# Head norm of a recurrent mixer: the bonus tiles loaded during the scan, gated by GpSimd and VectorE, their shift added by ScalarE

## The reference

```python
sa = einsum('bhij,bhj->bhi', state, kk_t)
state = state * w_t - sa * b_t + v_t * k_t           # one step per token
y_t = einsum('bhij,bhj->bhi', state, r_t)
...
y = (y - mean) * rsqrt(var + GN_EPS) * ln_w + ln_b    # head norm, per token and head
bonus = sum(r * k * r_k) * v                          # per head
y = y + bonus
return (y * silu(gate)) @ w_out
```

## Time and profile before

| what | value |
|---|---|
| time, median of 3 runs | 1241.23 us (1240.56 to 1241.37) |
| profiled execution: its own time, its span | 1244.49 us, 1242.7 us |
| TensorE, weight loads busy | 94%, 73% of the span |
| VectorE, ScalarE, GpSimd busy | 61%, 50%, 39% |
| TensorE's granted clock, mean over the span | 0.968 |
| DMA, mean | 96 GB/s |

### The profile page before, as it was taken

The page is one execution under the profiler, slowest core; times in us unless marked ns, Lnnn a source line. Parts: engine busy times, 40 slices in busy tenths (PEclk is TensorE's granted clock), DMA queues, the critical chain, the costliest instruction groups (busy, mean ns, idle before and its releaser), DMA issues.

```text
span 1242.7 us, 19541 instructions
## 1 busy us (share of the span) xinstructions
PE 1166.4 (94%) x7570; PEld 902.0 (73%) x7570; DVE 753.6 (61%) x1179; ACT 620.0 (50%) x1034; POOL 485.5 (39%) x391
## 2 busy tenths in 40 slices
PE   5899899998986999899999998999999999999997
PEld 4665667787872778677777776877888888867666
DVE  4775997894458346467666665274295234557763
ACT  4767453634553445466556464363122244465655
POOL 1432334456650444333323343443554445532321
PEclk9999899998896999899999999999999999999988
DMA  7742244536113253212222222522333333222111
GB/s 239 250 118 68 62 109 136 153 93 158 43 63 114 68 178 103 68 52 70 66 69 68 68 69 84 153 86 85 86 102 102 88 99 102 85 70 67 51 35 68
DMA packets 198941, 119.49 MB, mean 96 GB/s; under 512 B 27773, under 2 KB 187206, under 8 KB 198598
## 3 DMA queue, kind: packets, MB, share of 16 engines
q1 hardware_dynamic: 196256, 115.95, 32.1%
q10 hardware_dynamic: 2598, 2.33, 0.6%
HBM read 103.06 MB, written 15.20 MB: 95 GB/s over the span
## 4 chain that ended last, share of the span: by engine, by line
PE 41%; issue 30%; POOL 13%; DVE 12%; ACT 2%; DMA 1%; POOLq 0%; SPq 0%; ACTq 0%; DVEq 0%
POOL b_w_lo L562 13%; PE banks L645 10%; PE banks L647 10%; PE banks L646 10%; DVE b_problems L2129 1%; DVE b_sum_squares L2127 1%; PE banks L652 1%; PE banks L1220 1%; DVE b_a_lo L1989 1%; PE banks L893 1%; DVE b_suffix L2580 1%; PE banks L1248 1%; DMA b_spread_heads<-spread_heads 1%; PE banks L912 1%; DVE b_sum_squares L2062 1%
## 5 line engine op out<-in xcount | busy, mean ns | idle before, releaser
L562 POOL TENSOR_TENSOR b_w_lo<-b_w_raw,b_w_hi 128x512 fp32r<-128x512 f32 x320 | 429.5, 1363 | 711.6 <-ACT b_w_hi L1318 711.4
L645 PE MATMUL banks<-b_a_lo,b_w_hi 128*128 128x512 f32 x1280 | 527.4, 412 | 21.1 <-POOL b_w_lo L562 8.3
L647 PE MATMUL banks<-b_a_hi,b_w_lo 128*128 128x512 f32 x1280 | 508.3, 397 | 0.0
L646 PE MATMUL banks<-b_a_hi,b_w_hi 128*128 128x512 f32 x1280 | 507.2, 396 | 0.0
L645 PEld LDWEIGHTS banks<-b_a_lo,b_w_hi 128*128 128x128 f32 x1280 | 245.1, 191 | 101.8 <-issue 21.6
L1318 ACT ACTIVATE b_w_hi<-b_w_raw 128x1024 fp32r<-128x1024 f32 x160 | 168.8, 1055 | 250.3 <-PE banks L647 244.9
L647 PEld LDWEIGHTS banks<-b_a_hi,b_w_lo 128*128 128x128 f32 x1280 | 244.9, 191 | 53.7
L646 PEld LDWEIGHTS banks<-b_a_hi,b_w_hi 128*128 128x128 f32 x1280 | 245.8, 192 | 44.7
L1725 ACT ACTIVATE b_exps<-banks,b_stats 128x128 f32<-128x128 f32 (+3 forms) x64 | 33.2, 524 | 61.1 <-DVE b_stats L2370 61.1
L1659 ACT ACTIVATE b_a_hi<-b_x_t,b_params 128x512 fp32r<-128x512 f32 x48 | 33.9, 719 | 54.1 <-DVE b_x_t L2255 53.6
L2255 DVE TENSOR_TENSOR b_x_t<-b_x_t,banks 128x512 f32<-128x512 f32 x32 | 22.0, 687 | 60.2 <-PE banks L647 60.2
(11 more groups left out here) (314 smaller groups left out, 1513.7 us busy)
## 6 DMA issues: line engine op xcount, KB each, us to landing
b_w_raw<-rw_w_in SPq DMA_DIRECT2D x32, 512.0 KB, 4.4
b_w_raw<-da_w_in SPq DMA_DIRECT2D x32, 512.0 KB, 4.0
b_w_raw<-w_in_a SPq DMA_DIRECT2D x32, 512.0 KB, 4.0
b_w_raw<-pe_w_gate SPq DMA_DIRECT2D x16, 512.0 KB, 3.9
d_ple<-b_ple_out SPq DMA_DIRECT2D x16, 256.0 KB, 4.7
b_w_raw<-rw_w_out SPq DMA_DIRECT2D x8, 512.0 KB, 4.8
b_ple_in<-d_ple SPq DMA_DIRECT2D x2, 2048.0 KB, 10.4
b_w_raw<-da_w_out SPq DMA_DIRECT2D x8, 512.0 KB, 4.0
```

What stands on the lines that cost most here:

```text
L562: m = pool.tensor_tensor(WLO[:, u % 2, ks], WRAW[:, u, ks], WHI[:, u % 2, ks].bitcast(F32), ALU.subtract)
L645: pe.matmul(dst, hi, a_lo[:, k_act, :], start=first, stop=False)
L646: pe.matmul(dst, hi, a_hi[:, k_act, :], start=False, stop=False)
L647: return pe.matmul(dst, lo, a_hi[:, k_act, :], start=False, stop=last)
```

## The change

Four things change together.

1. **ScalarE adds the norm's shift** to a bonus tile in `bonus_out`, with one activation in place, before the tile is written to DRAM. It waits for its own activation before it issues the write.
2. **The bonus tiles are loaded during the scan**, one by one, into buffers of the scan that are no longer read: tiles 0 to 5 over the blocks of chunks 0 to 5 (`b_blocks`), tiles 6 and 7 over half of `b_nk_rows`. SP waits for TensorE's products of chunks 3, 5 and 5 before them. The one transfer of 2 MB behind the scan is gone.
3. **GpSimd gates tiles 0 to 3**: three in the iteration of chunk 5, one in that of chunk 6.
4. **VectorE gates tiles 4 to 7**, with a multiplication alone, in front of its wait for the roots. The loop over tiles has no bonus operation any more.

```diff
--- before.py
+++ after.py
@@ -279,8 +279,9 @@
-    BVT, SPREADH2, SPREADHR2, RK2, RKS2, RKC2 = phase([
-        ("bonus_v", [P, NT, TOK]), ("spread_heads2", [P, 2, P]), ("spread_heads2_r", [P, 2, P], F32R),
+    GATED = 4
+    SPREADH2, SPREADHR2, RK2, RKS2, RKC2 = phase([
+        ("spread_heads2", [P, 2, P]), ("spread_heads2_r", [P, 2, P], F32R),
...
+    def bonus_home(j):
+
+        at = TRI0[:, j] if j < 2 else TRI1[:, j - 2] if j < 6 else NKR[:, 1, 4 * (j - 6):4 * (j - 6) + 4]
+        return at.rearrange("p j t -> p (j t)") if j < 6 else at.rearrange("p j h d -> p (j h d)")
...
+        def load_bonus(j):
+            sp.dma_start(bonus_home(j), D_BV[j]).then_inc(sem(f"bonus_in{j // 4}"), 16)
+
+        sp.wait_ge(sem("u_mm"), 4)
+        for j in range(4):
+            load_bonus(j)
+        sp.wait_ge(sem("u_mm"), 6)
+        for j in range(4, 6):
+            load_bonus(j)
+        sp.wait_ge(sem("s_mm"), 6)
+        for j in range(6, NT):
+            load_bonus(j)
         sp.wait_ge(sem("v_placed"), 2 * 2 * NC)
         sp.dma_start(XT[:, :, :], D_XT.rearrange("j p t -> p j t")).then_inc(sem("x_spilled"), 16)
         sp.wait_ge(sem("y_even"), 2 * NC)
         sp.wait_ge(sem("y_odd"), 2 * NC)
-        sp.dma_start(BVT[:, :, :], D_BV.rearrange("j p t -> p j t")).then_inc(sem("gn_in"), 16)
...
+        def gate_bonus(j):
+            pool.wait_ge(sem(f"bonus_in{j // 4}"), 64)
+            pool.tensor_tensor(bonus_home(j), bonus_home(j), GT[:, j, :], ALU.mult).then_inc(sem("bonus_gated"), 1)
+            pool.wait_ge(sem("bonus_gated"), j + 1)
...
+            if c == NC - 3:
+                for j in range(3):
+                    gate_bonus(j)
+            if c == NC - 2:
+                gate_bonus(3)
...
         def bonus_out(j):
             act.wait_ge(sem("bonus_v"), j + 1)
+            own.step(act.activation(TMP[:, 2 + j % 2, :], TMP[:, 2 + j % 2, :], ACT.Identity, bias=prm(LN_B, j)))
             act.dma_start(D_BV[j], TMP[:, 2 + j % 2, :]).then_inc(sem(f"bv_out{j % 2}"), 16)
...
-        act.wait_ge(sem("gn_in"), 32)
+        act.wait_ge(sem("gn_in"), 16)
...
         def gated_bonus(j):
-            own.step(stt(out=BVT[:, j, :], in0=BVT[:, j, :], scalar=prm(LN_B, j), in1=GT[:, j, :], op0=ALU.add, op1=ALU.mult))
+            own.step(tt(bonus_home(j), bonus_home(j), GT[:, j, :], ALU.mult))
...
-            tt(YT[:, j, :], YT[:, j, :], BVT[:, j, :], ALU.add).then_inc(sem("gn_done"), 1)
-
-        dve.wait_ge(sem("gn_in"), 32)
-        for j in range(4):
-            gated_bonus(j)
+            tt(YT[:, j, :], YT[:, j, :], bonus_home(j), ALU.add).then_inc(sem("gn_done"), 1)
+
+        dve.wait_ge(sem("bonus_in1"), 64)
+        for j in range(GATED, NT):
+            gated_bonus(j)
+        dve.wait_ge(sem("bonus_gated"), GATED)
...
         for k in range(NT):
-            if k + 4 < NT:
-                gated_bonus(k + 4)
             if k + 2 < NT:
                 gn_scale(k + 2)
```

## The result

The changed kernel takes 1245.66 us (median of 15 executions, 1237.8 to 1250.3) where the kernel before takes 1239.5 (15, 1233.8 to 1241.9): ratio 1.0038, interval 1.0024 to 1.0051, 4.7 us slower. (The 4.7 us are the ratio's 0.38%; the two medians lie 6.2 us apart.) The forecast was 1240.5 with a range from 1237.6 to 1243.4. A repeat of both gave 1.0038 again (1.0021 to 1.0056).

The account below looks back on a forecast made before the run. TensorE, busy 94%, bounds dense stages; VectorE's solve ends last in value and gate slots, and VectorE bounds the head norm. 2.2 + 0.4 + 0.1 - 3.4 = -0.7 us from 1241.2 gives 1240.5, range 1237.6 to 1243.4.

Parts of the forecast that it names:

- Part 1: Head norm: VectorE bounds it, and moving bonus work out shortens it; 3.4 us gain taken, between 2.1 and 4.5.
- (a): Head norm, before the roots' wait: four plain multiplications start earlier and run shorter; combination of the roots 0.62 us earlier.
- (b): Head norm, loop over tiles: four bonus operations of 0.78 us leave VectorE's loop, saving 3.12 us.
- (c): Head norm, TensorE's output projection: earlier low parts gain 2.1 to 4.5 us by where the clock rises; 3.4 taken.
- Part 2: Value and gate slots: activation and write issue hold ScalarE's queue; solve 2.2 us later, 0.4 more at the scan's start.
- The late write: Value slots: write 0 goes out 2.8 us later but lands in time at 2.1 us; priced at nothing.
- Rival B: Value slots: late writes take 5.7 us and delay VectorE's bonus 4 by 2.9; 1243.4 or 1244.7 us; chance 0.10.
- Part 3: Scan: bonus loads find SP's queue nearly free, GpSimd's gatings delay placings; 0 to 0.3 us loss, 0.1 taken.

Follow-up runs that it names:

- the loads alone: Kernel before with only the eight bonus-tile loads moved into the scan, VectorE shifting and gating all tiles in the old places: 1.0014 and 1.0015 of before.
- the shift in the scan: Changed kernel without activation before the writes; ScalarE shifts tiles 0 to 3 in scan chunks 4 and 5, VectorE tiles 4 to 7: 0.9991, 0.9977 of before.
- five buffers: Changed kernel with five buffers in place of two for bonus tiles on their way to DRAM, ScalarE's activation kept: 1.0015 of the kernel before, 1240.2 us.
- Shift alone: Kernel before with ScalarE's shift activation ahead of each bonus write, VectorE only multiplying in its old places: 1.0044 of before, 5.5 us.
- four gatings by GpSimd in the head norm: Kernel before, bonus loads behind the scan; tiles 4 to 7 shifted by ScalarE behind the roots, gated by GpSimd: 0.9993 and 0.9977, 1237.5 and 1237.6 us.

## Why the prediction was wrong

**Part 1, the head norm: right.** (a) 0.62 us was forecast; from the first square to the combination of the roots it is 12.17 before and 11.52 after, 0.65. That this fits so well is partly luck. From the last weighting of a centred tile to the combination the three profiles of the kernel before take 4.34, 3.81 and 4.73 us, by how long VectorE waits for the head table's transfer, and the changed kernel 3.69 and 3.70: 0.1 to 1.0 is saved. (b) 3.12 forecast, 3.15 measured (19.54 from combination to the end of the last low part, now 16.39). (c) 3.4 was taken; it is 4.4, at the upper end, since the clock is back at 2.4 GHz from 403.0 us on, before the last tiles. The same distance from the first square to the first residual tile, 29.0 to 29.15 us, stands in all six profiles with this head norm. That it reaches the end was not shown by one pair of kernels alone: between the loads alone (1.0014, 1.0015) and the shift in the scan (0.9991, 0.9977) lie 3.8 us, and both have the loads.

**Part 2, ScalarE's queue: right in size.** 2.2 + 0.4 = 2.6 us were forecast; with the ring cut by five buffers, 2.6 us remain (give or take the 2 us of a comparison; the profile's 2.3 us at the gate's last low part, counted from bonus 1, say the same without that spread). The path behind was not the one forecast: the solve did not end last any more, but TensorE's gate slots and the late load of the turned blocks did, and for TensorE's lower clock there, with which 2.5 to 2.8 us more pass from the low part to the last gate tile, the prediction had no term.

**The late write: the step that failed.** The prediction put it so: "Write 0 now goes out at about 216.5 [...]. At 2.1 us it lands at 218.6, in time. I price it at nothing". It went out at 217.30 and landed at 222.75. The row on which it should have rested was there: the very same write took 5.7 us in the kernel before, and it had hidden 5.2 of them. The median of the eight landings says nothing about this one, because the long ones are not chance but the writes that meet a weight load. "Seven of eight writes took about 2.1" is misread from it: in order the eight took 5.7, 2.9, 2.0, 2.2, 2.0, 3.9, 2.0 and 2.0 us, and the first three places read 5.5, 2.9, 2.0 in both other profiles of that kernel. A write moved by some 2 us can also come under the load that it had missed: with five buffers, writes 1 to 3 go out 1.9 to 2.1 us later than before and take 4.5, 4.7 and 4.7 us in place of 2.9, 2.0 and 2.2, with 0.52 MB of weights on queue 1 beside each. That five buffers take 2.9 us off is the price of the ring by the timed runs (1.0038 to 1.0015, intervals that overlap); the profiles, counted from bonus 1, have 3.6 and 2.2 us at bonus 4. Rival B had the mechanism with 0.10, and its +2.9 for bonus 4 is near both; it lacked the laps, the clock and the scan's loads. Each lap starts from the one before: ScalarE's copies wait for the late bonus operation, so the next write is later still. A ring's price is its lap against the time it has, lap by lap: 3.66 us of work (213.64 to 217.30) and a landing of 2.0 to 5.45 make laps of 9.2, 5.8 and 8.3 us, where the writes of the kernel before went out 6.6 us apart (the first at 213.71, the fourth at 233.43). So the three waits, 7.9 us in sum, make 3.6 of lateness: the short lap gives some back, and a wait is no delay where the engine would have waited for TensorE anyway.

By the Trainium skill, "DMA: Bandwidth & Descriptors" (Latency and other measured facts), the fixed part of a transfer grows with the load on memory. The rows fit it, 5.45 us against 2.02, but do not part it from what they show more plainly, sixteen engines already taken (97.6%).

**Part 3, the scan: mis-sized.** GpSimd's gatings cost what was forecast (3.97 for three, 1.27 for one) and are hidden. But 0.1 was taken for the scan, and the loads cost 1.8 (0.5 to 3.0), at least in part through TensorE's instructions. "Behind them on SP's queue stands only the reload of x" looked at one queue; the engines behind the queues are shared with all.

**The sum by the measured terms**: 2.6 (queue) + 2.9 (ring) + 1.8 (loads) - 4.4 (head norm) = +2.9 us, where 4.7 was measured with an interval of 3.0 to 6.3. The lateness of 9.6 us at the scan's first copies is partly refunded: while the scan's start waits, TensorE's instructions arrive, and its gaps for them between 284 and 372 us shrink from 5.6 us in the profile before (3.7 and 6.7 in its repeats) to 1.8 (1.7 in the repeat). How much of that refund one execution gets is what varies, and it was not separated; the 1.8 us that the sum lacks lie within what two comparisons of one kernel differ by. Shift alone (5.5) in place of queue and ring gives the same sum. So do the profiles: the first residual tile comes at 406.66, 403.86 and 404.40 us in the three of the kernel before and at 409.50 and 406.46 in the two of the changed kernel, 3.0 later in the mean.

## What to carry to other kernels

Before an operation is put in front of a DMA write, look up which write frees which buffer, and who needs it next: if the write closes a ring, compare the ring's lap with the slot, and take the landing of that write under its own neighbours on the DMA engines, never the median. A transfer that is moved into a stage "with free queues" shares its engines with the instruction loads of TensorE; where a stage has thousands of small matmuls, that is a cost. The cheapest place for extra work is an engine idle at that moment: the shift in the scan's idle ScalarE, or four gatings by GpSimd in the head norm, give 1237.5 to 1238.1 us, some 2 us under the kernel before and 6 to 8 under the changed one.

## What the runs showed of the hardware

Three things were not expected. TensorE's instruction loads (16 KB each) fall behind beside 256 KB transfers that run for 2.8 us: one load in each profile of the loads alone comes 4.8 to 4.9 us after the one before, 3.3 to 4.6 without, and gaps of 0.3 to 0.6 us follow, which end 1.2 to 1.7 us after a load. Start and end of a scan that depends on them vary between executions of one program, one step of it by 4.9 us (10.69 to 15.55).

And VectorE's operations with two inputs in SBUF were slower while GpSimd ran its four multiplications (381.07 to 386.92): the combination of the roots took 1.66 us (0.75 without) and two adds 0.76 and 1.16 (0.68 without), while the scalings from PSUM took 0.67. The four GpSimd multiplications took 5.85 us beside VectorE, where 1.27 each stands in the scan of the changed kernel. The Trainium skill, "GPSIMD Engine Reference" (Specifications), says that the two share their way to SBUF and clash where VectorE reads two inputs there; these rows agree.
